# Paired projections for the sample tile, and three edits to the paged attention, in a two-layer hybrid decoder step

## The reference, cut to what matters

```python
z = _rmsnorm(x, g_pre) @ w_in            # 1024 -> 384 + 256 + 32 + 512 + 128 + 128 + 256 + 16 + 256 + 256 + 256
(cq, ckv, kpe, gate_mla, gq, gk, gv, gg, gate_gla, mq, gate_mem) = _split_in(z)
q   = _rope_tail(_rmsnorm(_rmsnorm(cq, g_qa) @ w_uq, g_mla_q), pos)
ckv = _rmsnorm(ckv, g_kva)
...
def page_step(carry, inp):               # sample tokens, 32 cached pages of 128 positions each
    c_blk, kpe_blk = cache_ckv[layer, phys], cache_kpe[layer, phys]
    k  = _mla_keys(c_blk, kpe_blk, pos, w_uk, g_k)      # up-projection, rmsnorm, rotation of the tail
    sc = jnp.einsum('bthd,bphd->bhtp', q, k) * MLA_SCALE
    return _online_update(carry, sc, c_blk)             # running maximum, sum and latent
```

## Time and profile before

| | |
|---|---|
| median of three runs | 2830.61 us |
| profiled execution, its own time | 2829.48 us |
| its span | 2827.7 us |
| tensor engine, busy | 2774.8 us, 98% |
| vector engine, busy | 1890.2 us, 67% |
| scalar engine, busy | 880.6 us, 31% |
| mean granted clock of the tensor engine | 0.996 of 2.4 GHz |

### The profile page before, as it was taken

The page is one execution under the profiler, slowest core; times in us unless marked ns, Lnnn a source line. Parts: engine busy times, 40 slices in busy tenths (PEclk is TensorE's granted clock), DMA queues, the critical chain, the costliest instruction groups (busy, mean ns, idle before and its releaser), DMA issues.

```text
span 2827.7 us, 54687 instructions
## 1 busy us (share of the span) xinstructions
PE 2774.8 (98%) x18037; PEld 1641.3 (58%) x18037; DVE 1890.2 (67%) x3801; ACT 880.6 (31%) x1903; POOL 329.6 (12%) x467
## 2 busy tenths in 40 slices
PE   8999999999999999999999999999989999999999
PEld 5666677764455555555466667777545555555554
DVE  3566655557798878886245666555578887888842
ACT  1333333332333333331013333333323333333300
POOL 0111000002011111110010000000111111111100
PEclk9999999999999999999999999999999999999999
DMA  7222222326334444543532222232353444445422
GB/s 285 71 65 68 70 72 73 72 67 177 101 104 132 125 117 125 169 135 132 210 122 59 66 69 70 72 74 72 108 143 102 124 118 133 114 138 179 119 99 86
DMA packets 528941, 313.72 MB, mean 111 GB/s; under 512 B 360009, under 2 KB 512146, under 8 KB 525586
## 3 DMA queue, kind: packets, MB, share of 16 engines
q1 hardware_dynamic: 526912, 309.41, 38.1%
q10 hardware_dynamic: 1746, 0.81, 0.1%
HBM read 287.63 MB, written 89.60 MB: 133 GB/s over the span
## 4 chain that ended last, share of the span: by engine, by line
PE 86%; DVE 9%; ACT 2%; issue 1%; DMA 0%; POOL 0%; SPq 0%; DVEq 0%; ACTq 0%
PE ps L1918 29%; PE ps L1512 13%; PE ps L1997 8%; PE ps L1932 4%; PE ps L1949 4%; PE ps L1746 4%; PE ps L1506 3%; PE ps L1711 2%; PE ps L1771 2%; PE ps L1518 2%; PE ps L1523 2%; PE ps L1937 1%; ACT U L730 1%; PE ps L1718 1%; DVE w_in L1396 1%
## 5 line engine op out<-in xcount | busy, mean ns | idle before, releaser
L875 ACT ACTIVATE w_in<-ps 128x512 f32<-128x512 f32 x512 | 305.7, 597 | 726.3 <-PE ps L1918 719.8
L1918 PE MATMUL ps<-w_uk,region 128*128 128x512 f32 x1040 | 473.5, 598 | 0.0
L1396 DVE TENSOR_REDUCE w_in<-w_in 128x8 f32<-128x512 f32 x512 | 351.3, 686 | 72.2 <-ACT w_in L875 56.6
L1512 PE MATMUL ps<-w_in,xT 128*128 128x256 f32 (+6 forms) x1360 | 379.0, 432 | 2.1 <-DMA w_in<-in_w_in 1.6
L1512 PEld LDWEIGHTS ps<-w_in,xT 128*128 128x128 f32 (+1 forms) x1360 | 247.2, 186 | 113.0 <-issue 69.2
L1918 PEld LDWEIGHTS ps<-w_uk,region 128*128 128x128 f32 x1040 | 187.4, 191 | 211.1 <-issue 210.3
L1918 PE MATMUL ps<-w_uk,xT 128*128 128x512 f32 x672 | 309.0, 604 | 0.0
L604 POOL TENSOR_TENSOR rs<-us,mhalf 128x1 f32<-128x1 f32 (+4 forms) x132 | 130.9, 991 | 1334.3 <-DVE us L1034 730.1
L1918 PEld LDWEIGHTS ps<-w_uk,xT 128*128 128x128 f32 x672 | 122.8, 193 | 134.4 <-issue 134.1
L1918 PE MATMUL ps<-w_uk,W 128*128 128x512 f32 x336 | 151.7, 593 | 0.5 <-ACT w_in L875 0.5
L1746 PE MATMUL ps<-region,W 96*128 96x512 f32 (+3 forms) x384 | 147.1, 495 | 0.1
(11 more groups left out here) (403 smaller groups left out, 4079.3 us busy)
## 6 DMA issues: line engine op xcount, KB each, us to landing
pages_by_quarter<-in_cache_ckv SPq DMA_DIRECT2D x512, 128.0 KB
region<-pages_by_quarter SPq DMA_DIRECT2D x80, 512.0 KB, 4.0
region<-in_cache_ckv SPq DMA_DIRECT2D x320, 128.0 KB, 2.2
w_in<-pages_by_quarter SPq DMA_DIRECT2D x48, 512.0 KB, 4.1
w_in<-in_cache_ckv SPq DMA_DIRECT2D x192, 128.0 KB, 2.2
w_in<-in_w_in SPq DMA_DIRECT2D x16, 1240.0 KB, 11.1
mix_quarters<-xn SPq DMA_DIRECT2D x16, 512.0 KB, 3.7
region<-in_cache_kpe SPq DMA_DIRECT2D x512, 16.0 KB
```

Source lines behind the costliest of these rows:

```text
L875: tell(act.activation(sqb[j % 4], ps[:, j if k == 0 and j < 2 else 2 + j % 2, :], ACT.Square), s.pkn_sq, np_)
L1396: tell(dve.tensor_reduce(pst[:, 0, j * H:j * H + H], heads(sqb[j % 4], H), X, ALU.add), s.pkn_red, np_)
L1512: ins = mm(out, xT[:, k, 0:T], w_in[:, k, c0:c0 + w], start=k == 0, stop=k == KD - 1)
L1918: ins = mm(ps[:, key_bank(k, j), :], page[:, o_:o_ + P], w_uk[:, c, :], start=c == 0, stop=c == 1)
```

## The change

1. `project_pair`: in the sample tile two projections are issued alternately, one into partitions 0 to 63 and one into 64 to 127. GLA's values go with the memory queries (bank 5, both halves), `ckv` with `cq` (bank 2 below, bank 3 above). The two halves of the query product (L1711) are arranged in the same way. The readers of `mq`, `cq` and of the second half of the queries take partitions 64 to 127.
2. Their places: the pair with `mq` is issued at head 6 of prompt tile 7; at head 7 stand `project_T` for the sample tile's GLA queries and keys. Three steps of the output gates stand ahead of the transposition of `ck`, one behind the transposition of `cq`, four behind GLA.
3. `dg` is a matrix of ones times the maxima, and `maxima_over` is a transposition of it.
4. `scores_of` issues the rotary products first, then the pages'.
5. The new tokens' values alternate between banks 4 and 5, each product waits for the copy two before, and the table is (1, 7), (2, 0), (2, 2) to (2, 6), (3, 0). `pz` is made at (1, 4).

```diff
-NEW_VALUES = [(1, 6), (1, 7), (2, 0), (2, 1), (2, 2), (2, 3), (2, 4), (3, 0)]
+NEW_VALUES = [(1, 7), (2, 0), (2, 2), (2, 3), (2, 4), (2, 5), (2, 6), (3, 0)]
...
+                    else:
+                        own(act.activation(sq[0:TS, 0:4 * QK], ps[0:TS, 2, 0:4 * QK], ACT.Square))
+                        tell(act.activation(sq[0:TS, 4 * QK:8 * QK], ps[TS:2 * TS, 3, 0:4 * QK], ACT.Square), s.q_sq, n)
...
-                    if k == 1 and j == 5:
+                    if k == 1 and j == 4:
                         dve.wait_ge(s.pnT_ps, L + 1)
...
-                        tell(cp(acc[0:TS, b, :], ps[0:TS, 5, 0:RW]), s.acc_ready, DB * L + b)
+                        tell(cp(acc[0:TS, b, :], ps[0:TS, 4 + b % 2, 0:RW]), s.acc_ready, DB * L + b)
...
-                    tell(ts(dg, ident[:], sm[:, 1:2], None, ALU.mult), s.pd_ready, n0)
+                    tell(ts(dg, ones[:], sm[:, 1:2], None, ALU.mult), s.pd_ready, n0)
...
+                def project_pair(lo, w_lo, hi, w_hi):
+
+                    for k in range(KD):
+                        a_lo = mm(lo, xT[:, k, 0:TS], w_in[:, k, w_lo[0]:w_lo[0] + w_lo[1]], start=k == 0, stop=k == KD - 1)
+                        a_hi = mm(hi, xT[:, k, 0:TS], w_in[:, k, w_hi[0]:w_hi[0] + w_hi[1]], start=k == 0, stop=k == KD - 1)
+                    return a_lo, a_hi
...
                     if n:
-                        project_T(ps[:, 4, 0:T], T, O_GQ, GKD)
-                        project_T(ps[:, 4, P:P + T], T, O_GK, GKD)
+                        if pm_:
+                            project_T(ps[:, 4, 0:T], T, O_GQ, GKD)
+                            project_T(ps[:, 4, P:P + T], T, O_GK, GKD)
...
-                        project(ps[0:T, 2, 0:R + ROPE], T, O_CKV, R + ROPE).then_inc(s.ckv_ps, 1)
+                        if pm_:
+                            project(ps[0:T, 2, 0:R + ROPE], T, O_CKV, R + ROPE).then_inc(s.ckv_ps, 1)
+                        else:
+                            a_ckv, a_cq = project_pair(ps[0:TS, 2, 0:R + ROPE], (O_CKV, R + ROPE), ps[TS:2 * TS, 3, 0:QR], (O_CQ, QR))
+                            a_ckv.then_inc(s.ckv_ps, 1)
+                            a_cq.then_inc(s.cq_ps, 1)
...
-                    else:
-                        project(ps[0:T, 3, 0:QR], T, O_CQ, QR).then_inc(s.cq_ps, 1)
...
+                    if not pm_:
+                        project_gates(0, 3)
+                    pe.wait_ge(s.ck_ready, n + 1)
...
-                        project_gates(0, 1)
+                        project_gates(3, 4)
...
+                    else:
                         for c in range(3):
-                            ins = mm(ps[0:T, 2 + e, 0:4 * QK], cqT[:, c, 0:T], w_uq[:, c, 4 * QK * e:4 * QK * e + 4 * QK], start=c == 0, stop=c == 2)
+                            for e in range(2):
+                                ins = mm(ps[TS * e:TS * e + TS, 2 + e, 0:4 * QK], cqT[:, c, 0:T], w_uq[:, c, 4 * QK * e:4 * QK * e + 4 * QK], start=c == 0, stop=c == 2)
...
                             if h == 6:
-                                project_gv(t + 1)
+                                if t + 1 < TP:
+                                    project_gv(t + 1)
+                                else:
+                                    project_gv_mq()
                             if h == 7:
-                                project_mq(t + 1)
+                                if t + 1 < TP:
+                                    project_mq(t + 1)
+                                else:
+                                    project_T(ps[:, 4, 0:TS], TS, O_GQ, GKD)
+                                    project_T(ps[:, 4, P:P + TS], TS, O_GK, GKD)
...
                         if b == 0:
                             pe.wait_ge(s.pz_ready, L + 1)
-                        else:
-                            pe.wait_ge(s.acc_ready, DB * L + b)
-                        mm(ps[0:TS, 5, 0:RW], pz[:, b, :], ck[0:TS, :], start=True, stop=True).then_inc(s.acc_ps, 1)
+                        if b >= 2:
+                            pe.wait_ge(s.acc_ready, DB * L + b - 1)
+                        mm(ps[0:TS, 4 + b % 2, 0:RW], pz[:, b, :], ck[0:TS, :], start=True, stop=True).then_inc(s.acc_ps, 1)
...
-                    mm(ps[:, 7, 384:512], ones[:], dg, start=True, stop=True).then_inc(s.pmb_ps, 1)
+                    tp(ps[:, 7, 384:512], dg, ident[:]).then_inc(s.pmb_ps, 1)
```

More of the change, by code:

```diff
@@ L701, in _ @@
                     act.wait_ge(s.gvmq_ps, 2 * n + 2)
-                    tell(act.activation(qk[0:T, 0, 0:MW], ps[0:T, 6, 0:MW], ACT.Square), s.mq_ss, n)
+                    tell(act.activation(qk[0:T, 0, 0:MW], ps[0:T, 6, 0:MW] if pm_ else ps[TS:2 * TS, 5, 0:MW], ACT.Square), s.mq_ss, n)
                     act.wait_ge(s.ckv_ps, n + 1)
@@ L1656, in _ @@
                         project_part(ps[0:T, 3, 0:QR], T, O_CQ, QR, 1, KD).then_inc(s.cq_ps, 1)
-                    pe.wait_ge(s.ck_ready, n + 1)
-                    for c in range(2):
-                        ins = tp(ps[:, 2, c * P:c * P + T], chunk(ck[0:T, 0:R], c), ident[0:T, 0:T])
-                    ins.then_inc(s.cT_ps, 1)
                     def project_gates(k0, k1):
@@ L1668, in project_gates @@
                         return ins
+                    if not pm_:
+                        project_gates(0, 3)
+                    pe.wait_ge(s.ck_ready, n + 1)
+                    for c in range(2):
+                        ins = tp(ps[:, 2, c * P:c * P + T], chunk(ck[0:T, 0:R], c), ident[0:T, 0:T])
+                    ins.then_inc(s.cT_ps, 1)
                     def intra_gla():
@@ L1706, in _ @@
                     else:
-                        project_gates(0, 1)
+                        project_gates(3, 4)
                     pe.wait_ge(s.cqT_evac, n + 1)
-                    for e in range(2):
+                    if pm_:
+                        for e in range(2):
+                            for c in range(3):
+                                ins = mm(ps[0:T, 2 + e, 0:4 * QK], cqT[:, c, 0:T], w_uq[:, c, 4 * QK * e:4 * QK * e + 4 * QK], start=c == 0, stop=c == 2)
+                    else:
                         for c in range(3):
-                            ins = mm(ps[0:T, 2 + e, 0:4 * QK], cqT[:, c, 0:T], w_uq[:, c, 4 * QK * e:4 * QK * e + 4 * QK], start=c == 0, stop=c == 2)
+                            for e in range(2):
+                                ins = mm(ps[TS * e:TS * e + TS, 2 + e, 0:4 * QK], cqT[:, c, 0:T], w_uq[:, c, 4 * QK * e:4 * QK * e + 4 * QK], start=c == 0, stop=c == 2)
                     ins.then_inc(s.q_ps, 1)
@@ L1926, in scores_of @@
                         pe.wait_ge(s.qt_ready, L + 1)
+                    for c in range(2):
+                        for half in range(0, P, 64):
+                            for r in range(2):
+                                w = slice(64 * r, 64 * r + 64)
+                                mm(ps[half:half + 64, r, P * c:P * c + P], rotT[w, c, half:half + 64], qrz[w, 2 * r:2 * r + 2, 64 * b:64 * b + 64], start=c == 0, stop=False)
                     for j in range(G):
@@ L1931, in scores_of @@
                                 o_ = (j % 2) * R + c * P + half
-                                mm(ps[half:half + 64, j // 4, so_:so_ + 64], page[:, o_:o_ + 64], qt[:, c, 64 * b:64 * b + 64], start=c == 0 and j % 4 == 0, stop=False)
-                    for c in range(2):
-                        for half in range(0, P, 64):
-                            for r in range(2):
-                                w = slice(64 * r, 64 * r + 64)
-                                ins = mm(ps[half:half + 64, r, P * c:P * c + P], rotT[w, c, half:half + 64], qrz[w, 2 * r:2 * r + 2, 64 * b:64 * b + 64], start=False, stop=c == 1)
+                                ins = mm(ps[half:half + 64, j // 4, so_:so_ + 64], page[:, o_:o_ + 64], qt[:, c, 64 * b:64 * b + 64], start=False, stop=c == 1 and j % 4 == 3)
                     ins.then_inc(s.ps_ps, 1)
```

17 lines of the change are left out of this document (11 added, 6 removed).

## The result

| | before | after |
|---|---|---|
| median | 2830.11 us (4 runs, 2829.28 to 2831.42) | 2796.5 us (4 runs, 2795.93 to 2797.0) |
| ratio, 95% interval | | 0.9881 [0.9864, 0.9898] |
| profiled execution, own time | 2829.48 us | 2795.93 us |
| span | 2827.7 us | 2794.1 us |

A forecast was written before the change was run, and what follows sets the result against it. The tensor engine, busy 98% of the span, was taken as the bound, except where it waits for another engine. +1 - 7.0 - 6.4 - 18.5 = -31 us on 2829.5 gave 2798.6, forecast as 2800 us, range 2788 to 2812.

The forecast's parts named there:

- pairs and their places: Sample tile: 1.1 us a layer arrives, 2.2 in all; clock falls cost 3.4; together +1 us.
- maxima by a turning: Page groups: one tensor instruction instead of two, 0.11 us in each of 64 groups, 7.0 us saved.
- rotary scores first: Page groups: three shape changes instead of four, 0.10 us in each of 64 groups, 6.4 us saved.
- new tokens' values: First page groups: 13.2 us of waits and 5.3 us of slow clock go, 18.5 us saved together.
- A: New tensor-engine wait in the sample tile for the gate rank's copy, forecast at 2.5 us a layer.
- B: New tensor-engine wait in the sample tile for the gates (g_ready), forecast at 2.0 us a layer.
- C: New tensor-engine wait in the sample tile for the sample queries (qn_ready), forecast at 3.5 us a layer.
- two falls of four chances: Sample tile, both layers: clock drops to 0.50 behind two of four new waits, some 1.8 us each, +3.4 us.
- the distance: From prompt tile 7's gate rank to L1827's counterpart: forecast 1.1 us a layer shorter before clock falls.
- The wait left at (2, 5): Tensor-engine wait for the new tokens' values copy that remains, forecast at 0.65 us a layer.
- The three falls: Stretches at clock 0.50 behind the old values' waits, one in the first layer, two in the second; 5.3 us saved.
- busy share: Tensor engine's busy part of the span, forecast to go from 98% to about 97%.

The follow-up runs named there:

- e1: The changed kernel with the sample tile's projections, their places and readers as before (no pairs): 2791.68 us, ratio 0.9863.
- e2: The changed kernel with maxima_over as the product of ones with the diagonal again: 2803.46 us, ratio 0.9903.
- e3: The changed kernel with the pages' products first and the rotary ones behind them, as before: 2807.4 us, ratio 0.9916.
- e4: The changed kernel with the new tokens' values in bank 5 alone, at the old places, pz at (1, 5): 2819.62 us, ratio 0.9958.
- e9: The changed kernel with seven products more a layer that nobody reads, ahead of three tensor-engine waits in the sample tile: 2791.68 us, ratio 0.9858.
- e7: The changed kernel with half of the rotary products ahead of the pages' products, half behind: 2815.85 us, ratio 0.9951.
- e5: The changed kernel with project_T behind tile 7's last product again and two early gate steps ahead of the gates' sum: 2787.43 us, ratio 0.9853.
- e11: The changed kernel with two waits filled, three vector-engine moves and both rotation tables scaled on GpSimd: 2802.01 us, ratio 0.9896.

## Why the prediction was right

**The sum.** The two profiled executions differ by 33.6 us; I had 31. Part of the agreement is luck: the pairs cost 4 us more than I took, and about as much came from places that I had not counted (1.3, 1.6 and up to 1.7 us, below). By stretches of the two traces:

| step | forecast | measured |
|---|---|---|
| pairs and their places | +1 (-19.6 to +6.4) | +5.2 (2.4 and 2.8); e1: 4.8 |
| maxima by a turning | -7.0 | -7.0 (e2) |
| rotary scores first | -6.4 | -8.8 (0.137 a group, e3); e3 as a whole: -10.9, the rest not shown to be the order's |
| new tokens' values (measured with a fall behind group 0) | -18.5 | -20.3 in the traces (below); e4: -23.1 |
| not forecast | | -1.3 in the prologue, -1.6 at the second layer's start |

**Pairs.** The mechanism was right step by step: A 2.5 us (2.46 measured), B 2.0 (1.86), C 3.5 (3.44), the side-by-side halves, and that 8 to 9 of 9.8 us a layer turn into waits. The term was mis-sized in the clock: I took two falls of four chances behind A and B. There were three, behind A in both layers and behind B in the second, and two more behind C. The one behind A in the first layer lasted 6.8 us, twice the 3.4 us of the others, and my 1.8 us each came from falls of that shorter kind. The measured +5.2 lies near the upper end of the bounds. e9 shows that the clock is the cause: without falls the distance is 0.8 and 0.9 us shorter than in the kernel before, where I had 1.1.

**Maxima.** Right to 0.1 us, from two neighbouring rows.

**Rotary scores.** The sign and the count of changes were right; one change less is worth 0.137 us, not the 0.10 that the keys' row shows. e7 has the parts: sixteen 64-row products take 0.60 us in one piece and 0.76 in two halves, and the values behind them 1.89 instead of 1.84. The Trainium skill says in TensorEngine Tiling (Array Packing), Key Properties, that a change of the tiling mode drains the engine. That each change costs time agrees with it, 0.137 us for one (e3) and 0.285 for two (e7); that the time is a drain no run here shows.

**New tokens' values.** The wait left at (2, 5) was 0.48 us for 0.65. Not forecast is the 0.5 us a layer that `values` waits for the scalar engine in these groups (0.2 in one layer before). The three falls went with the waits. From L1827's counterpart to the third turning of maxima it takes 10.2 and 11.3 us less, 21.5 together. By the prices of e2 and e3, 1.3 of them belong to the maxima and the order, which leaves 20.3; up to 1.7 of that, half of 3.4, is the fall at 690 us in the kernel before, which followed no wait and which I had not counted.

**What was missed.** 1.3 us before the sample tile (a fall of the clock at 113 us that the profiled execution after does not have) and 1.6 us for a weight transfer at the second layer's start. Both helped, and neither comes from an edit that I could name. One sign did not come: the tensor engine's busy share stayed at 98%, where I had put 97. The new waits A to C add 15.5 us of idle, about what the values' waits gave up (13.5), and a product at the lower clock counts as busy for longer.

## What to carry to other kernels

Where the tensor engine is busy 98% of the span, the 2% mark the places where its list does not set the end; work taken away there turns into waits, so follow the other engine's chain through the stage first, and fill the new waits with work that is there anyway (e5: 9 us faster than the change). A wait costs more than its length when the clock falls behind it, and idle products are worth their time then. Before work is moved to an engine that seems idle, or behind a signal, look at what it shares and at who waits for the next signal.

## What the runs showed of the hardware

- Waits of 1.75 to 3.44 us on the tensor engine were often followed by a granted clock of 0.50 for 3.4 or 6.8 us (17.1 around one of 9.7 us, in e11), in which four 128x512 key instructions took 3.65 us instead of 1.98. It does not follow each wait (none behind 1.75 and 2.51 us in the first layer before, nor behind 1.86 in the first layer after), and the clock also fell at 690 us before, behind 8-column products and no wait. Products that nobody reads, put into the waits, kept it at 1.00 through the tile (e9).
- GpSimd held the vector engine up (e11): a vector product of two inputs in the on-chip memory, 0.28 us alone, took 2.32 us beside a GpSimd product of 2.89 us, and four copies took 4.25 instead of 1.25. The Trainium skill (GPSIMD Engine Reference, section Specifications) lists the interfaces as shared, with contention for vector instructions with two such inputs or in a 2-port performance mode. The trace agrees for the product; the copies, with one input, slowed too, and no run here shows in which mode they ran.
- Two float32 products of 272 and 256 columns in the two column halves took the time of the wider one, 7.8 us for 32 instructions of each.
- A change of the tile shape between products cost 0.14 us: 0.137 for one more in a group (e3), 0.285 for two (e7).
